# Late input-projection blocks of a hybrid decoder step, dealt in threes over all eight samples of the paged attention

## What is computed

```python
h = _rms_norm(x, lp['norm_pre_mix'])
proj = h @ lp['w_in']                       # columns of all mixers and gates
...
ckv_past = cache_ckv[l][page_table].reshape(b_s, past_len, MLA_KV_LORA)   # 16 pages of 128 rows per sample
kpe_past = cache_kpe[l][page_table].reshape(b_s, past_len, MLA_ROPE_DIM)
...
s = (einsum('bthc,bsc->bhts', q_lat, ckv) + einsum('bthr,bsr->bhts', q_pe, kpe)) * scale
probs = softmax(concatenate(scores, axis=-1), axis=-1)
part = einsum('bhts,bsc->bthc', probs[..., start:stop], ckv)
```

## Time and profile before

| | |
|---|---|
| median of 3 runs | 2015.82 us (2013.42 to 2021.24) |
| the profiled execution, its own time | 2015.85 us |
| its span in the trace | 2014.0 us |
| PE busy | 1894.6 us (94%) |
| DVE, ACT, POOL busy | 609.8, 447.7, 112.5 us |
| mean granted clock of PE | 0.95 of full speed |

### The profile page before, as it was taken

The page is one execution under the profiler, slowest core; times in us unless marked ns, Lnnn a source line. Parts: engine busy times, 40 slices in busy tenths (PEclk is TensorE's granted clock), DMA queues, the critical chain, the costliest instruction groups (busy, mean ns, idle before and its releaser), DMA issues.

```text
span 2014.0 us, 26383 instructions
## 1 busy us (share of the span) xinstructions
PE 1894.6 (94%) x10428; PEld 1409.8 (70%) x10428; DVE 609.8 (30%) x1376; ACT 447.7 (22%) x955; POOL 112.5 (6%) x190
## 2 busy tenths in 40 slices
PE   6999899999999999999999988998999998999997
PEld 5576577766776767777766755777678766777775
DVE  1331256422203325330033213563322033343301
ACT  2233123103113231111132331321121123311100
POOL 1003000001001010000010030000000011100000
PEclk9999879979999999999999996898799999999999
DMA  8512313017345624343164133220163455333431
GB/s 294 172 58 79 116 32 117 22 43 285 126 146 191 243 93 146 131 140 123 59 236 146 37 80 118 73 73 22 57 270 128 145 208 213 113 138 132 144 126 45
DMA packets 67053, 257.82 MB, mean 128 GB/s; under 512 B 8561, under 2 KB 36658, under 8 KB 39666
## 3 DMA queue, kind: packets, MB, share of 16 engines
q1 hardware_dynamic: 55154, 201.69, 28.6%
q0 software_dynamic: 11360, 54.21, 7.2%
q10 hardware_dynamic: 416, 0.25, 0.0%
HBM read 246.92 MB, written 9.19 MB: 127 GB/s over the span
## 4 chain that ended last, share of the span: by engine, by line
PE 87%; DVE 7%; issue 3%; ACT 2%; DMA 1%; SPq 0%; DVEq 0%; POOL 0%; ACTq 0%; POOLq 0%
PE banks L782 37%; PE banks L811 15%; PE banks L733 8%; PE banks L766 6%; PE banks L730 5%; PE banks L789 5%; PE banks L840 3%; PE banks L738 3%; DVE projected L1832 2%; DVE work L1832 1%; PE banks L1028 1%; DVE o_branches L1832 1%; PE banks L1383 1%; PE banks L999 1%; PE banks L1402 1%
## 5 line engine op out<-in xcount | busy, mean ns | idle before, releaser
L782 PE MATMUL banks<-h_normed,weight_ring 128*128 128x288 f32 x1888 | 459.4, 406 | 1.1 <-ACT h_normed L1465 1.1
L782 PEld LDWEIGHTS banks<-h_normed,weight_ring 128*128 128x128 f32 x1888 | 358.6, 190 | 100.5 <-ACT h_normed L1465 1.5
L811 PE MATMUL banks<-h_normed,weight_ring 128*128 128x288 f32 x1024 | 287.5, 433 | 6.8 <-ACT values_by_token L1628 6.8
L811 PEld LDWEIGHTS banks<-h_normed,weight_ring 128*128 128x128 f32 x1024 | 204.8, 204 | 68.6 <-ACT values_by_token L1628 8.9
L782 PE MATMUL banks<-work,weight_ring 128*128 128x288 f32 (+1 forms) x960 | 226.8, 399 | 1.8 <-issue 1.8
L782 PEld LDWEIGHTS banks<-work,weight_ring 128*128 128x128 f32 x960 | 182.2, 190 | 46.1 <-issue 2.6
L1465 ACT ACTIVATE work<-banks 128x512 f32<-128x512 f32 (+9 forms) x194 | 92.1, 475 | 322.5 <-PE banks L738 83.1
L766 PE MATMUL banks<-h_normed,weight_ring 128*128 128x288 f32 x480 | 123.8, 409 | 0.0
L1832 DVE TENSOR_TENSOR squares<-squares 128x288 f32<-128x288 f32 (+2 forms) x40 | 20.3, 508 | 329.4 <-ACT squares L1503 329.2
L766 PEld LDWEIGHTS banks<-h_normed,weight_ring 128*128 128x128 f32 x480 | 88.5, 190 | 30.9 <-issue 9.2
L840 PE MATMUL banks<-h_normed,weight_ring 128*128 128x288 f32 x288 | 80.4, 439 | 25.2 <-DMA weight_ring<-in_w 18.7
(11 more groups left out here) (308 smaller groups left out, 1927.1 us busy)
## 6 DMA issues: line engine op xcount, KB each, us to landing
weight_ring<-in_w SPq DMA_DIRECT2D x172, 1024.0 KB, 4.8
work<-in_mem_k POOLq DMA_DIRECT2D x12, 1024.0 KB, 11.4
work<-in_mem_v POOLq DMA_DIRECT2D x12, 1024.0 KB, 8.9
work<-in_pool SPq DMA_DIRECT2D x128, 80.0 KB, 2.0
weight_ring<-in_pool SPq DMA_DIRECT2D x64, 80.0 KB, 2.0
projected<-in_mem_k POOLq DMA_DIRECT2D x4, 1024.0 KB, 23.5
projected<-in_mem_v POOLq DMA_DIRECT2D x4, 1024.0 KB, 6.4
weight_ring<-in_pool POOLq DMA_DIRECT2D x32, 80.0 KB, 2.3
```

The source lines that it names most:

```text
L782: last = mm(ps[:, bank, 0:width], block_of(first + k), rhs(k), start=k == 0, stop=k == n - 1)
L811: last = mm(ps[:, BANK[g], 0:N], block_of(t[2] + k), H[:, k, :] if t[0] == "gate" else O[:, 2 * n + k, :], start=k == 0, stop=k == t[3] - 1)
```

## The change

`fill(6)` for the first four samples becomes `fill(3)` for the first seven, and two more `fill(3)` stand in the last pair's chain, around `maxima_back`. The block count stays 48 (14 x 3 + 2 x 3). ACT's six `late_out` calls are moved to follow.

```diff
@@ PE, loop over the samples
                         turns(b, 4)
-                        fill(6 if b < 4 else 0)
+                        fill(3 if b < NB - 1 else 0)
                         if b + 1 < NB:
                             turns(b + 1, 0)
                             turns(b + 1, 1)
                         scores(b)
-                        fill(6 if b < 4 else 0)
+                        fill(3 if b < NB - 1 else 0)
                         if b % 2 == 0 and g >= 0:
                             attend(g)
                     g = NB // 2 - 1
                     maxima(g)
+                    fill(3)
                     maxima_back(g)
+                    fill(3)
                     attend(g)
                     outputs(g)
@@ ACT
-                            if (b, j) in ((1, 1), (2, 1), (2, 3), (3, 1), (4, 1), (4, 3)):
+                            if (b, j) in ((2, 1), (3, 1), (4, 1), (6, 1), (7, 1)):
                                 late_out()
                         if b % 2 == 0 and b:
                             exps(b // 2 - 1)
                     exps(NB // 2 - 1)
+                    late_out()
                     wait("mla_o")
```

## The result

| | before | after |
|---|---|---|
| median of the runs | 2016.94 us (6 runs, 2012.64 to 2023.68) | 2079.80 us (6 runs, 2078.80 to 2085.94) |
| profiled execution, its own time | 2015.85 us | 2078.80 us |
| span | 2014.0 us | 2076.9 us |
| PE busy | 1894.6 us | 1891.6 us |
| PE not busy (span less busy) | 119.4 us | 185.3 us |

The changed kernel is slower: 1.0317 times the time before, 95% interval 1.0292 to 1.0341. The forecast was 2088 us, range 2064 to 2112.

What follows compares the result with a forecast made beforehand. The prediction took PE to bound the kernel, with 87% of the chain of waits. Page waits 76.2 plus restarts 8.8, less covered waits 7.8 and clock 5.0, gave 72.2 us on 2015.85: 2088 us, range 2064 to 2112.

Steps and rivals of the forecast that it cites:

- the four page waits: Ahead of samples 5 and 6 in each layer, PE stands still for late pages: 76.2 us lost.
- four restarts at the low clock: After each page wait PE restarts at 1.2 GHz, 2.2 us each: 8.8 us lost.
- old waits covered: In samples 4 to 6 and the last chain, fills cover PE's waits: net 3.9 us a layer, 7.8 us gained.
- clock given back: In the last pair's stretches more work keeps PE's clock up: 5 us gained, taken between 0 and 13.
- Sample 5's chain: From sample 3's second fill to `turns(5, 0)`: 21.9 us needed, 3.7 us covered, so PE stands still 18.2 us.
- Sample 6's chain: From tile 12, two blocks into the fill ahead of `turns(6, 0)`: 20.0 us needed, 0.5 us covered, 19.5 us standing still.
- Sample 7's pages: Fetched by POOL behind sample 5's, landing about 19 us after them, while PE waits for sample 6: no wait added.
- rival 3: PE's clock stays at 1.2 GHz from the first restart to the attention's end: 25 us a layer, 2140 us; chance 0.06.
- The rule that I weighed: For page-number reads, the skill's 200 ns a register gives 3.2 us for 16, each wait some 6 us shorter, 2064 us.
- Rival 1: At `turns(5, 0)` and `turns(6, 0)` the pages come in time: 2003 us, with all of the clock 1995; chance 0.03.
- Rival 2: Page numbers are cheap, read ahead of the gate or faster; each wait loses about 9 us: 2052 us; chance 0.04.
- Rival 4: The order's effect is nil, something unseen sets the pace of the page attention: 2016 us; chance 0.02.

Runs made afterwards that it cites:

- e8_before_read: The kernel before, with page numbers read ahead of the gates and nothing else: 2017.61 us, 1.0003 times the kernel before.
- e4_tail_only: The kernel before, with sample 3's second fill of six blocks moved as 3 and 3 around the last pair's `maxima_back`: 2000.31 us, 0.9910 times the kernel before.
- e1_read_first: The changed kernel, with page numbers of samples 5, 6 and 7 read ahead of the wait for the late tile: 2047.74 us, 1.0145 times the kernel before.
- e2_no_fetch: The changed kernel, with samples 5 and 6 using the pages of samples 1 and 2, their own not fetched: 1998.71 us, 0.9902 times the kernel before.
- e9_gate_earlier: Against the kernel before: blocks spread, also inside `attend`, page numbers read ahead of the gates, tile 12 done at the end of sample 3: 1988.68 us, 0.9860 times.

## Why the prediction was right, point by point

The sign, the mechanism and the places were right, and the time was 8 us below the forecast. One of the stated signs was missed: PE's busy time was to grow by some 4 to 10 us, and it fell by 3.0. The terms of the sum, on the profiled executions (2078.80 - 2015.85 = 62.95 us, forecast 72.2):

| term | forecast | measured | from |
|---|---|---|---|
| the four page waits | +76.2 | +74.0 | PE's timeline |
| four restarts at the low clock | +8.8 | +6.6 | below |
| old waits covered | -7.8 | -8.1 | idle account |
| clock given back | -5.0 | -9.6 | what is left: 5.5 in the page attention, 4.1 outside it |

**Sample 5's chain.** Forecast 21.9 us from gate to transposes and 3.7 us of cover. Measured in layer 0: 175.71 to 197.51 us is 21.8 us, less 18.13 is 3.7 us.

**Sample 6's chain.** Forecast 20.0 us and 19.5 us of standing still. Measured: 19.06 and 19.21 us; from SP's first page number (214.9) to the transposes (234.37) are 19.5 us. I had added 0.8 us for a slow issue on SP seen in layer 1 of the kernel before; layer 1's wait was not longer by that.

**Sample 7's pages** were off the path, as said: no row of DVE or PE waits for them.

**Covered waits.** 8.1 for 7.8 us. The 0.2 us a layer that I took off for a late copy did not come: the samples with short fills have the same 0.30 us wait as before.

**Restarts.** I took 2.2 us each. They can be read from the time between the start of sample 5's or 6's transposes and the next fill. Undisturbed, in sample 3, it is 2.83 us (171.32 to 174.15). After the waits it is 4.36 (197.51 to 201.87), 4.64, 4.55 and 4.35 us, together 6.6 us more, just under the least that I had allowed (6.8). The clock was back after 3.0 to 3.7 us, where the row that I went by the earlier trace rows showed 4.8.

**The clock given back** is the term furthest off: "Between 0 and 13 I take 5 us gained." As the remainder it measured 9.6 us. The page attention holds 5.5 us of it: PE's busy time there rose by 1.1 us (166.6 to 167.7) with 6.6 us of restarts in it. So for the stage that I priced, 5 us was about right, though with slow stretches that I had not counted on (see rival 3). Another 4.6 us lie in the stage behind it in layer 0, where the order is the same, and the remaining stages took back 0.4. I had no term for that stage. Whether the change set its clock there is open: it took 251.8 to 264.0 us in the eleven profiled executions, and e8_before_read, with the PE order of the kernel before, had 257.0. As far as the runs show, this part of the miss is chance, and without it the forecast would have been 4.6 us nearer. I had chosen low in my 0 to 13 since I counted on the idle pieces of over 1 us that remain to bring the clock down; in layer 1 of the changed kernel and in layer 0 of e4_tail_only they did not, in the 25 us read above.

**The rule that I weighed.** By the rows a page number cost 0.56 to 0.63 us; by the Trainium skill (Runtime: NRT & Kernel Launch, "Instruction fetch mechanics"), which puts a `TENSOR_LOAD` at about 200 ns a register, the time would by my estimate have been 2064 us. It was 2079.8, and e1_read_first measured the reads alone: 35.9 us less waiting for 4 x 16 numbers, 0.56 us a number. The measurement decides. The load itself is 266 to 283 ns in the rows, and the register operation and the assertion behind each add 147 and 18 ns. That is 0.43 to 0.45 us of the 0.56 to 0.63; the rest of a number's cost has no row of its own.

**Rivals.** Rival 1 fell: the gates left 3.7 and 0.5 us of cover, not 20. e2_no_fetch shows what it would have been worth, 1999 us where I wrote 1995 to 2003. Rival 2 fell: the reads stood behind the gate and at full price. Rival 3 fell: the clock came back after each restart, though in layer 0 it dropped once more in sample 5, from about 207.4 to 214.2 us (stretches of 1 us between show 0.50, and the fill at 213.17 takes 2.14 us for 1.62). Rival 4, no effect at 2016 us, fell with the time.

## What to carry to other kernels

A filler block may be more than filler: before moving it, look for every wait on the count that it raises, and set the time from that count to its user against the work that now stands between. Here 48 blocks looked alike, but the 24th and the 32nd each opened transfers that need 20 us and more. What needs no gate, such as reading addresses into registers, belongs ahead of the wait, though it gains only where somebody waits for what is fetched (32 us in e1_read_first, nothing in e8_before_read); and a gate's lead is to be measured with the other queues' transfers running beside it.

## What the runs showed of the hardware

For transfers whose address is read at run time, reading the addresses took about as long as the transfers: 16 page numbers took 8.9 us on SP and 10.1 us on POOL, and 16 transfers of 80 KB took some 8 to 9 us to issue and 2.2 us more for the last to land.

The granted clock of PE made a difference larger than the idle time that was moved. Six blocks in the last pair's chain took 2.6 us of idle time and 7.0 us of busy time out of the page attention of the profiled run, and 18 us out of the median (2018.48 to 2000.31). Which clock a stretch gets also varies between executions where the order is the same: from the output matrices to the norm behind the mixers (236.28 to 493.12 us before, 272.96 to 525.23 us after) layer 0 took 256.8 us at a mean of 0.87 before the change, 252.3 us at 0.88 after it, and 264.0 us at 0.84 in e9_gate_earlier. What decides the level in that stage was not tried.
